# Half of the attention weights turned by VectorE and two DMAs instead of TensorE, in a 16-head attention stage

## The chip, the core and the metric

The kernel runs on one core of one Trainium2 chip. The time is device microseconds (us) of that core, for one whole execution of the program. Three timed runs of the kernel before took 1644.7 to 1644.83 us, median 1644.71. The profile shows a separate execution of the same program with a span of 1645.5 us.

## What is computed

The reference is a two-layer block over 512 positions of width 1024, followed by a second block, all in fp32. The change lies in the attention of the first layer, which in the reference is, cut to what matters:

```python
mod_x = silu_c @ mod_w[i] + mod_b[i]                 # 6144 values, used as shifts, scales and gates
q = (rmsnorm(h @ w_dq, g_q) @ w_uq)                  # 16 heads of 64 + 32 (the 32 are rotated)
k = concat([ckv @ w_uk, k_pe]); v = ckv @ w_uv       # 768 keys: 256 of the context, 512 of x
s = einsum('bqhd,bkhd->bhqk', q, k) * scale          # 512 queries x 768 keys, for each head
p = softmax(s, axis=-1)
o = einsum('bhqk,bkhd->bqhd', p, v)                  # 64 columns for each head
x = x + g1 * (o @ w_o)
```

The rest of the reference (two feed-forward blocks, a long convolution, a state-space branch and a pooling branch) is computed by parts of the program that the change does not touch.

## The kernel before

Each engine runs a list of instructions written out by hand; engines wait for each other through counted semaphores (`S["name"]`), and each list is executed in its order. A matrix product in fp32 precision is three products of rounded parts (`mm3`, lines 2442 to 2446): high by high, high by low, low by high.

The attention stage handles one head after another; with `head(h)` TensorE finishes head h and computes the scores of head h+1. For TensorE (lines 2836 to 2867) it is: transposes of the weights of head h; four score tiles of head h+1, each of 128 queries by 768 keys, with pieces of projections and more transposes between them; in even heads the key projection of the next pair; then `value(h)`, the product of the turned weights with V. A score tile takes two of the four PSUM banks 0 to 3, so tile qt+2 waits until the exponential of tile qt has read its banks (`sexp`, line 2772).

For each score tile VectorE takes the row maximum (`maximum`, line 3568), ScalarE the exponential with its row sum (`exponential`, line 3085), and VectorE the reciprocal of the sum (`inverse_sum`, line 3575), before it goes to the next maximum. The weights are multiplied by the reciprocal by GpSimd for tiles 0 to 2 (line 2374) and by ScalarE for tile 3 (line 3114). They stand with queries on the partitions (`PR`, two buffers, for even and odd heads); the product with V needs keys on the partitions, so TensorE turns 24 blocks of 128x128 for each head into PSUM (`turn_blocks`, line 2780), and ScalarE copies them to `PT` (`turn_copy`, line 3094). At the end of a head VectorE writes the low part of the head's output (`out_lo`, line 3581), which needs `value(h)` and ScalarE's high part.

VectorE has two more jobs there. It computes rows of the modulation, each a product of a 128x1024 piece of `mod_w` with the vector c and a sum (`mod_rows`, line 3519). Rows 0 to 27 are computed in heads 0 to 13, two in each; SyncE loads each piece (512 KB) into one of two buffers MR0 and MR1 once the row two before it is done (`mod_load`, line 2194). And between heads 14 and 15 it computes angles for the state-space branch (`prepare_angles`, line 3672). After the heads comes the output projection "wo", in eight tiles: `linear("wo", j)` waits until the residual of tile j-2 is added by VectorE (line 2457).

All DMAs of this stage are issued by SyncE, in the order of its list (lines 2244 to 2264). Which head is which matters: heads with h mod 4 equal to 1 carry the projection of the rotated part and heads with h mod 4 of 2 or 3 that of query pairs; heads 4, 8 and 12 have one such product only.

## Time and profile before

| | |
|---|---|
| median of 3 timed runs | 1644.71 us (1644.7 to 1644.83) |
| span of the profiled execution | 1645.5 us |
| TensorE busy | 1633.9 us, 99% |
| VectorE busy | 1043.6 us, 63% |
| ScalarE busy | 571.0 us, 35% |
| GpSimd busy | 1026.5 us, 62% |
| mean granted TensorE clock | 0.997 |
| DMA, mean over the span | 134 GB/s |

The profiled execution's own time is its span, 0.8 us above the median of the timed runs. The stage of the heads goes from 112.9 us, where head 0 begins, to 316.8 us, where the last product with V ends. Shares over the whole span say little of it: whether an engine is waited for there has to be read from that stretch. An idle time in square brackets stands before an instruction, with the engine and line that ended it.

### The profile page before, as it was taken

What the parts mean: (1) busy time and instruction counts of PE and PEld (TensorE: products, weight loads), DVE (VectorE), ACT (ScalarE), POOL (GpSimd) and SP (SyncE); (2) the same over time, 40 slices, a digit from 0 to 9 for tenths busy, and PEclk for the clock granted to TensorE, in tenths of its full rate; (3) what the DMA queues carried; (4) which work ended last, traced back from release to release, by engine and by line L of the source; (5) the groups of instructions that cost most, each with busy time, mean ns of one, the idle gap of its engine ahead of it and who ended that gap; (6) DMA issues with size and microseconds to landing.
All of it is one profiled execution on the core that took longest, in us unless ns stands there. A gap on an engine that the chain in (4) does not pass through costs nothing.

```text
span 1645.5 us, 24018 instructions
## 1 busy us (share of the span) xinstructions
PE 1633.9 (99%) x8950; PEld 1364.2 (83%) x8950; DVE 1043.6 (63%) x1537; ACT 571.0 (35%) x1017; POOL 1026.5 (62%) x656
## 2 busy tenths in 40 slices
PE   9999999999999999999999999999999999999998
PEld 7887778798888888889887798888888898888887
DVE  3567777677877865635487566655558359746173
ACT  3467777633233232203344243222222121123111
POOL 3455766656666766575579456666676645567663
PEclk9999999999999999999999999999999999999999
DMA  9234335232269863435322233344434253223332
GB/s 371 87 90 129 111 106 165 79 93 96 89 211 320 298 225 103 141 137 172 120 90 65 77 99 102 125 156 140 153 106 143 97 214 120 65 84 103 91 101 90
DMA packets 59095, 220.61 MB, mean 134 GB/s; under 512 B 6849, under 2 KB 9153, under 8 KB 55682
## 3 DMA queue, kind: packets, MB, share of 16 engines
q1 hardware_dynamic: 53826, 204.96, 38.2%
q10 hardware_dynamic: 5184, 14.49, 2.3%
q8 instruction: 57, 0.93, 0.2%
q14 instruction: 28, 0.23, 0.0%
HBM read 201.07 MB, written 14.16 MB: 131 GB/s over the span
## 4 chain that ended last, share of the span: by engine, by line
PE 95%; DVE 4%; ACT 0%; issue 0%; DMA 0%; DVEq 0%; SPq 0%; ACTq 0%
PE PS L2444 28%; PE PS L2446 28%; PE PS L2445 28%; PE PS L2821 3%; PE PS L2783 2%; PE PS L1012 1%; PE PS L2430 1%; PE PS L1785 1%; PE PS L2595 1%; DVE SC L3572 0%; DVE WA L1990 0%; PE PS L1791 0%; DVE MR L3522 0%; PE PS L2720 0%; PE PS L2721 0%
## 5 line engine op out<-in xcount | busy, mean ns | idle before, releaser
L2354 POOL TENSOR_TENSOR WL<-RAW,WH 128x1024 fp32r<-128x1024 f32 (+3 forms) x211 | 542.8, 2572 | 17.6
L2444 PE MATMUL PS<-HH,WH 128*128 128x512 f32 (+1 forms) x1340 | 507.5, 379 | 0.0
L2446 PE MATMUL PS<-HH,WL 128*128 128x512 f32 (+1 forms) x1340 | 502.9, 375 | 0.0
L2445 PE MATMUL PS<-HL,WH 128*128 128x512 f32 (+1 forms) x1340 | 502.9, 375 | 0.0
L2351 POOL TENSOR_SCALAR WH<-RAW 128x1024 fp32r<-128x1024 f32 (+3 forms) x211 | 239.4, 1134 | 287.8 <-PE PS L2446 276.5
L2444 PEld LDWEIGHTS PS<-HH,WH 128*128 128x128 f32 x1340 | 252.2, 188 | 50.7 <-issue 6.2
L2446 PEld LDWEIGHTS PS<-HH,WL 128*128 128x128 f32 x1340 | 252.2, 188 | 45.9
L2445 PEld LDWEIGHTS PS<-HL,WH 128*128 128x128 f32 x1340 | 252.3, 188 | 43.9
L2379 POOL TENSOR_SCALAR PR<-PR,SC 128x768 f32<-128x768 f32 x47 | 107.3, 2292 | 66.7 <-DVE SC L3579 66.3
L2444 PE MATMUL PS<-HIDH,WH 128*128 128x512 f32 (+1 forms) x396 | 145.3, 367 | 0.0
L2445 PE MATMUL PS<-HIDL,WH 128*128 128x512 f32 (+1 forms) x396 | 144.8, 366 | 0.0
L2446 PE MATMUL PS<-HIDH,WL 128*128 128x512 f32 (+1 forms) x396 | 144.7, 366 | 0.0
L2350 POOL TENSOR_TENSOR SC<-ONES 1x1 f32<-1x1 f32 x100 | 24.9, 249 | 180.1 <-PE PS L2446 177.7
L3278 ACT ACTIVATE ZG<-PS,PAR 128x512 f32<-128x512 f32 x44 | 34.3, 779 | 166.3 <-PE PS L2446 166.3
L2444 PEld LDWEIGHTS PS<-HIDH,WH 128*128 128x128 f32 x396 | 74.6, 188 | 12.6 <-issue 0.5
L2446 PEld LDWEIGHTS PS<-HIDH,WL 128*128 128x128 f32 x396 | 74.7, 189 | 12.1
L2445 PEld LDWEIGHTS PS<-HIDL,WH 128*128 128x128 f32 x396 | 74.7, 189 | 12.1
L3792 DVE SCALAR_TENSOR_TENSOR ZG<-PS,PAR,ZG 128x511 f32<-128x511 f32 x44 | 33.0, 750 | 72.2 <-ACT ZG L3278 71.9
L3572 DVE TENSOR_REDUCE SC<-PS 128x1 f32<-128x768 f32 x64 | 61.1, 955 | 23.1 <-PE PS L2446 22.5
L3681 DVE SCALAR_TENSOR_TENSOR X<-PS,MOD,X 128x512 f32<-128x512 f32 x26 | 19.5, 749 | 87.6 <-PE PS L2446 87.6
L3091 ACT ACTIVATE PR<-PS,SC 128x768 f32<-128x768 f32 x64 | 57.8, 903 | 44.3 <-DVE SC L3572 44.1
L3530 DVE CUSTOM_DVE_ANT_0 MRF<-MRF,PS 128x1024 f32<-128x1024 f32 x52 | 62.5, 1211 | 2.9 <-DMA MRF<-in_modw 2.7
(532 smaller groups left out, 2894.6 us busy)
## 6 DMA issues: line engine op xcount, KB each, us to landing
RAW<-in_wup SPq DMA_DIRECT2D x88, 512.0 KB, 3.6
MRF<-in_modw SPq DMA_DIRECT2D x52, 512.0 KB, 4.8
RAW<-in_wdn SPq DMA_DIRECT2D x32, 704.0 KB, 4.1
MR<-in_modw SPq DMA_DIRECT2D x28, 512.0 KB, 3.6
RAW<-in_whin SPq DMA_DIRECT2D x24, 512.0 KB, 3.5
MK<-in_modk SPq DMA_DIRECT2D x8, 1024.0 KB, 10.9
RAW<-in_wo SPq DMA_DIRECT2D x8, 512.0 KB, 4.2
hy_hs<-HST ACTq DMA_DIRECT2D x4, 1024.0 KB, 4.0
```

The lines of the kernel that those rows point to most:

```text
L2351: pool.tensor_scalar(WH[s][:, 0:n], raw[:, 0:n], 1.0, 0.0, ALU.mult, ALU.add).then_inc(tile_hi, 1)
L2354: pool.tensor_tensor(WL[s][:, 0:n], raw[:, 0:n], WH[s][:, 0:n].bitcast(F32), ALU.subtract).then_inc(tile_split, 1)
L2379: pool.tensor_scalar(PR[h % 2][:, qt, :], PR[h % 2][:, qt, :], RSUM[:, c:c + 1], None, ALU.mult).then_inc(S["pnorm"], 1)
L2444: pe.matmul(out, wh, xh, start=first, stop=False)
L2445: pe.matmul(out, wh, xl, start=False, stop=False)
L2446: return pe.matmul(out, wl, xh, start=False, stop=last)
L2821: m = pe.matmul(PS[VH * half:VH * half + VH, out_bank(h), 0:256], V[:, kt, v], PT[:, kt, tok(half)], start=kt == 0, stop=kt == 5)
L3091: act.activation(PR[h % 2][:, qt, :], wide(2 * (qt % 2), LK), ACT.Exp, bias=NMX[:, c:c + 1], scale=1.0, accum_out=SUMS[:, c:c + 1]).then_i ...
L3278: act.activation(buf[:, :], bank(first_bank(2 * o + half)), ACT.Identity, scale=par_at("fcw", i + (l * 3 * NUP + NUP + KF * half + o)), bi ...
L3530: dve.tensor_tensor_reduce(MRF[b][:, :], MRF[b][:, :], wide(6, D), 1.0, 0.0, ALU.mult, ALU.add, MOD[:, 16 + r:17 + r]).then_inc(S["mod_use ...
L3572: dve.tensor_reduce(NMX[:, c:c + 1], wide(2 * (qt % 2), LK), AX.X, ALU.max, negate=True).then_inc(S["smax"], 1)
L3792: link(dve.scalar_tensor_tensor(buf[:, 1:L], bank(bk)[:, 0:L - 1], w0, buf[:, 1:L], ALU.mult, ALU.add))
```

## The change

Of each head, query tiles 0 and 1 are no longer turned by TensorE (`BLOCKED = 2`). The exponential of these tiles writes its keys in another order: column c*192 + t*32 + j holds key 128t + 4j + c. VectorE then transposes the 32x32 blocks of each 128x768 tile in place (`block_turn`). SyncE writes both tiles to a buffer in HBM (`blocks_out`, 384 KB each), waits until both have landed and until the product with V of the head before is done, and reads them back with one DMA that puts 1024 pieces of 768 bytes on 128 partitions (`blocks_in`, 768 KB in all). The product with V reads these from `PB` and the turned tiles 2 and 3 from `PT`. TensorE turns 12 blocks for each head instead of 24, in three groups of four (`turn(h, 0)` and `turn(h, 1)` at the start, `turn(h, 2)` after the second score tile), and these wait for all of tiles 2 and 3, while before the first six waited for tile 2 only. ScalarE copies three times for each head instead of six.

The modulation rows are spread anew: rows 0 to 4 before head 0, rows 5 and 6 in head 0, two in each odd head up to 13, three in head 14 and four in head 15; none in even heads from 2 to 12. `prepare_angles` stands behind head 15. X is loaded again in two halves, at heads 14 and 15. Some semaphores are merged, with no change in what is waited for.

```diff
+BLOCKED = 2
+PRE_ROWS = 5
-        PT = r.put("PT", [P, 6, L])
+        PB = r.put("PB", [P, BLOCKED, 4, 6, 32])
+        PT = r.put("PT", [P, 6, P * (4 - BLOCKED)])
...
+            def blocks_out(h, qt):
+                sp.wait_ge(S["turned"], BLOCKED * h + qt + 1)
+                sp.dma_start(d_blocks[h % 2, qt, :, :], PR[h % 2][:, qt, :]).then_inc(S["blocks_out"], 16)
+            def blocks_in(h):
+                sp.wait_ge(S["pv"], h + 1)
+                sp.wait_ge(S["blocks_out"], 16 * BLOCKED * (h + 1))
+                sp.dma_start(PB[:, :, :, :, :].rearrange("p i m t j -> p (i m) (t j)"),
+                             d_blocks[h % 2].rearrange("i (m k) (c x) -> (k c) (i m) x", m=4, c=4)
+                             ).then_inc(S["blocks_in"], 16)
...
+            for r in range(4):
+                mod_load(16 + r)
+                if r == 1:
+                    head_weights(2)
+            for h in range(16):
...
+                if h % 2 and h < 15:
+                    mod_load(16 + PRE_ROWS + 1 + h)
+                    mod_load(16 + PRE_ROWS + 2 + h)
...
+                elif h == 14:
+                    sp.wait_ge(S["rope"], 512)
+                    x_again(0)
+                    mod_load(16 + EARLY - 7)
+                elif h == 15:
+                    mod_load(16 + EARLY - 5)
+                    mod_load(16 + EARLY - 4)
+                for qt in range(BLOCKED):
+                    blocks_out(h, qt)
+                if h > 13:
+                    mod_load(16 + EARLY + 3 * h - 48)
+                blocks_in(h)
+                if h == 0:
+                    for r in range(4, PRE_ROWS + 2):
+                        mod_load(16 + r)
+            x_again(1)
+            mod_load(16 + EARLY - 2)
+            mod_load(16 + EARLY - 1)
...
+            def turn(h, n):
+                if n == 0:
+                    pe.wait_ge(S["pnorm"], 3 * h + 2)
+                    if h == 0:
+                        pe.wait_ge(S["kready"], key_hi_at(0) + 2)
+                    else:
+                        pe.wait_ge(S["pt"], 4 * h + 1)
+                if n == 2:
+                    pe.wait_ge(S["pt"], 4 * h + 2)
+                for kt in (2 * n, 2 * n + 1):
+                    for qt in range(BLOCKED, 4):
+                        q = (kt % 2) * 256 + (qt - BLOCKED) * P
+                        m = pe.transpose(PS[:, 6 + n % 2, q:q + P], PR[h % 2][:, qt, kt * P:(kt + 1) * P], IDENT[:, :])
+                m.then_inc(S["s_tr"], 1)
...
+                pe.wait_ge(S["blocks_in"], 16 * (h + 1))
                 for kt in range(6):
-                    pe.wait_ge(S["pt"], 7 * h + kt + 2)
-                    for half in range(2):
-                        m = pe.matmul(PS[VH * half:VH * half + VH, out_bank(h), 0:256], V[:, kt, v],
-                                      PT[:, kt, tok(half)], start=kt == 0, stop=kt == 5)
+                    pe.wait_ge(S["pt"], 4 * h + kt // 2 + 2)
+                    pe.matmul(PS[0:VH, out_bank(h), 0:256].rearrange("p (i m j) -> p i m j", i=2, m=4), V[:, kt, v],
+                              PB[:, :, :, kt, :], start=kt == 0, stop=kt == 5)
+                    m = pe.matmul(PS[VH:2 * VH, out_bank(h), 0:256], V[:, kt, v], PT[:, kt, :], start=kt == 0, stop=kt == 5)
...
+                if qt < BLOCKED:
+                    out, src = out.rearrange("p (c t j) -> p c t j", c=4, t=6), src.rearrange("p (t j c) -> p c t j", t=6, c=4)
...
+            def block_turn(h, qt, i=0, per=0):
+                dve.wait_ge(S["pnorm"], i * (3 * per) + (3 * h + qt if h else qt + 1))
+                dve.transpose(PR[h % 2][:, qt, :], PR[h % 2][:, qt, :]).then_inc(S["turned"], 1)
...
                 if h < 15:
                     inverse_sum(h + 1, 3, i, per)
+                    block_turn(h + 1, 0, i, per)
...
                 if h % 2:
                     row(1)
+                if h in (14, 15):
+                    row(2)
+                if h == 15:
+                    row(3)
+                if h < 15:
+                    block_turn(h + 1, 1, i, per)
                 out_lo(h, i, per)
```

Two places show how the lists move: the start of head 0 on two engines, and the end of the heads on VectorE.

SyncE's list where the first modulation rows are loaded, before. MR is the buffer of a modulation row, RAW that of a weight tile.

```order
L2170 ISA [waits tile_split]
L2170 DMA RAW_53<-in_wheven 128x1280
L2196 ISA
L2197 ISA [waits s_mod_used]
L2197 DMA MR_93<-in_modw 128x1024
L2196 REGISTER_ALU
L2197 ISA [waits s_mod_used]
L2197 DMA MR_94<-in_modw 128x1024
```

The same place in the changed kernel. PR are the weights, PB their turned blocks.

```order
L2214 DMA MR_94<-in_modw 128x1024 [waits s_mod_used]
L2214 DMA MR_95<-in_modw 128x1024 [waits s_mod_used]
L2174 DMA RAW_53<-in_wheven 128x1280 [waits tile_split]
L2214 DMA MR_94<-in_modw 128x1024 [waits s_mod_used]
L2214 DMA MR_95<-in_modw 128x1024 [waits s_mod_used]
L2201 DMA pr_blocks<-PR_72 128x768 [waits s_turned] x2
L2207 DMA PB<-pr_blocks 128x8x192 [waits s_blocks_out,s_pv]
L2214 DMA MR_94<-in_modw 128x1024 [waits s_mod_used]
```

Four rows are loaded first, and the load of row 4, the last line, now stands behind the DMA that reads the blocks of head 0 back.

VectorE's list from the last reciprocal of head 0's scores, before. TENSOR_REDUCE is a maximum, here the first of head 1's scores; ISA with MR is a modulation row.

```order
L3579 RECIPROCAL SC<-SC 128x1 [waits s_sexp] x2
L3572 TENSOR_REDUCE SC<-PS 128x1 [waits s_s_ready]
L3522 ISA MR_93,SC<-MR_93,CB 128x1024 [waits s_mod_in0]
L3522 ISA SC 128x1
L3579 RECIPROCAL SC<-SC 128x1 [waits s_sexp]
```

The same place in the changed kernel.

```order
L3610 RECIPROCAL SC<-SC 128x1 [waits s_sexp]
L3625 STREAM_TRANSPOSE PR_72<-PR_72 128x768 [waits s_pnorm] x2
L3553 ISA MR_94,MOD<-MR_94,CB 128x1024 [waits s_mod_in0]
L3553 ISA MOD 128x1
L3553 ISA MR_95,MOD<-MR_95,CB 128x1024 [waits s_mod_in1]
L3553 ISA MOD 128x1
L3553 ISA MR_94,MOD<-MR_94,CB 128x1024 [waits s_mod_in0]
L3553 ISA MOD 128x1
L3603 TENSOR_REDUCE SC<-PS 128x1 [waits s_s_ready]
```

Two transposes and the modulation rows 2, 3 and 4 now stand ahead of the first maximum of head 1's scores.

VectorE's list from the last reciprocals of head 15's scores, before. HL is the low part of a head's output, S are the angles; the lines between the first and the last of the angles are left out here.

```order
L3579 RECIPROCAL SC<-SC 128x1 [waits s_sexp] x2
L3587 TENSOR_TENSOR HL<-PS,HH 64x256 [waits s_ohi] x2
L1398 TENSOR_SCALAR S_139<-PAR 128x16
...
L1507 TENSOR_SCALAR S_139<-S_139 128x16 [waits s_dchain]
L3587 TENSOR_TENSOR HL<-PS,HH 64x256 [waits s_ohi,s_s5d]
L3587 TENSOR_TENSOR HL<-PS,HH 64x256 [waits s_ohi]
```

The same place in the changed kernel; of the four modulation rows of head 15 the first is shown.

```order
L3610 RECIPROCAL SC<-SC 128x1 [waits s_sexp] x2
L3625 STREAM_TRANSPOSE PR_73<-PR_73 128x768 [waits s_pnorm]
L3553 ISA MR_95,MOD<-MR_95,CB 128x1024 [waits s_mod_in1]
L3553 ISA MOD 128x1
L3625 STREAM_TRANSPOSE PR_73<-PR_73 128x768 [waits s_pnorm]
L3618 TENSOR_TENSOR HL<-PS,HH 64x256 [waits s_ohi] x2
L3553 ISA MR_94,MOD<-MR_94,CB 128x1024 [waits s_mod_in0]
...
L3618 TENSOR_TENSOR HL<-PS,HH 64x256 [waits s_ohi] x2
L1402 TENSOR_SCALAR S_140<-PAR 128x16 [waits s_mod_used]
```

The low part of head 15's output stood behind the angles and now stands ahead of them, behind four modulation rows; two transposes with a modulation row between them have come in behind the reciprocals.

## Rows read from the trace of the kernel before

**Rows 1.** The page, chain that ended last, shares of the span.
```profile
PE 95%; DVE 4%; ACT 0%; issue 0%; DMA 0%; DVEq 0%; SPq 0%; ACTq 0%
```

**Rows 2.** Chain of waits, 200 to 235 us: start, length, engine, what.
```profile
208.23 1.02 PE PS L2783 x8
...
213.19 0.44 PE PS L2783 x4
```

**Rows 3.** Timeline of VectorE, head 7: start, length, engine, line, what, idle before.
```profile
210.35 0.96 DVE L3572 TENSOR_REDUCE SC<-PS 128x1 f32<-128x768 f32 x1 [0.58 <-PE PS L2446]
...
216.75 0.16 DVE L3579 RECIPROCAL SC<-SC 128x1 f32<-128x1 f32 x1 [1.06 <-ACT PR L3091]
216.89 0.96 DVE L3572 TENSOR_REDUCE SC<-PS 128x1 f32<-128x768 f32 x1
...
218.99 1.20 DVE L3522 CUSTOM_DVE_ANT_0 MR<-MR,CB 128x1024 f32<-128x1024 f32 x1
...
220.73 0.88 DVE L3587 TENSOR_TENSOR HL<-PS,HH 64x256 f32 x2 [0.53 <-ACT HH L3111]
222.16 0.96 DVE L3572 TENSOR_REDUCE SC<-PS 128x1 f32<-128x768 f32 x1 [0.56 <-PE PS L2446]
```

**Rows 4.** Timeline of VectorE, the first maximum in heads 1, 2, 5, 13, 14.
```profile
130.84 0.96 DVE L3572 TENSOR_REDUCE SC<-PS 128x1 f32<-128x768 f32 x1
...
142.16 0.88 DVE L3587 TENSOR_TENSOR HL<-PS,HH 64x256 f32 x2 [1.42 <-ACT HH L3111]
143.22 0.96 DVE L3572 TENSOR_REDUCE SC<-PS 128x1 f32<-128x768 f32 x1 [0.18 <-PE PS L2446]
...
182.99 0.96 DVE L3572 TENSOR_REDUCE SC<-PS 128x1 f32<-128x768 f32 x1 [0.56 <-PE PS L2446]
...
287.56 0.96 DVE L3572 TENSOR_REDUCE SC<-PS 128x1 f32<-128x768 f32 x1 [0.57 <-PE PS L2446]
...
300.05 0.96 DVE L3572 TENSOR_REDUCE SC<-PS 128x1 f32<-128x768 f32 x1 [0.80 <-PE PS L2446]
```

**Rows 5.** DMA issues of the page: KB each, median us from issue to landing.
```profile
RAW<-in_wdn SPq DMA_DIRECT2D x32, 704.0 KB, 4.1
MR<-in_modw SPq DMA_DIRECT2D x28, 512.0 KB, 3.6
...
hy_hs<-HST ACTq DMA_DIRECT2D x4, 1024.0 KB, 4.0
```

**Rows 6.** DMA issues by the DMA view, same columns.
```profile
X<-in_x SPq DMA_DIRECT2D x2, 1024.0 KB, 6.2
...
s_cs<-COW ACTq DMA_DIRECT2D x4, 256.0 KB, 2.1
```

**Rows 7.** Timeline of VectorE, start of head 0.
```profile
109.19 0.16 DVE L3579 RECIPROCAL SC<-SC 128x1 f32<-128x1 f32 x1 [1.87 <-ACT PR L3091]
115.04 0.96 DVE L3572 TENSOR_REDUCE SC<-PS 128x1 f32<-128x768 f32 x1 [5.69 <-PE PS L2446]
115.92 2.63 DVE L3522 CUSTOM_DVE_ANT_0 MR<-MR,CB 128x1024 f32<-128x1024 f32 x1
```

**Rows 8.** Timeline of TensorE, the last product with V and the fourth "wo" tile.
```profile
314.02 2.81 PE L2821 MATMUL PS<-PT,V 128*64 128x256 f32 x24
...
327.11 0.39 PE L2444 MATMUL PS<-HH,WH 128*128 128x512 f32 x1
```

**Rows 9.** Timeline of VectorE, end of the heads and "wo".
```profile
310.27 0.16 DVE L1398 TENSOR_SCALAR S<-PAR 128x16 f32<-128x16 f32 x1
...
318.11 0.88 DVE L3587 TENSOR_TENSOR HL<-PS,HH 64x256 fp32r<-64x256 f32 x2
...
320.60 0.75 DVE L3681 SCALAR_TENSOR_TENSOR X<-PS,MOD,X 128x512 f32<-128x512 f32 x1 [0.98 <-PE PS L2446]
321.87 0.75 DVE L3681 SCALAR_TENSOR_TENSOR X<-PS,MOD,X 128x512 f32<-128x512 f32 x1 [0.52 <-PE PS L2446]
...
330.39 0.74 DVE L3681 SCALAR_TENSOR_TENSOR X<-PS,MOD,X 128x512 f32<-128x512 f32 x1
```

More of the change, by code:

```diff
@@ L3123, in head @@
                 turn_copy(h, 0, i, per)
+                if h % 4 == 0 and per:
+                    mod_store(i)
                 for kt in range(1, 6):
[L3125 removed]
+                    if kt == 1 or kt == 3:
+                        turn_copy(h, (kt + 1) // 2, i, per)
                     if kt == 1 and h % 4 == 3 and h < 12:
@@ L3145, in head @@
                     query_hi(3)
-                if h % 2 and h < 14:
-                    mod_store(2 * h - 2, 4, i, 2 * per)
             rope_hi(0)
```

175 lines of the change are left out of this document (83 added, 92 removed).

## Prediction, written before the changed kernel ran

> **What bounds the kernel now.** I read the page first. The chain that ended last is TensorE for 95% of the span [rows 1], so a change pays if it takes work off TensorE and no other engine takes its place. Then the chain of waits in the stretch of the heads, for the price of what goes: a group of four transposes holds the chain 0.44 us, the first eight of a head 1.02 us [rows 2]. Then VectorE's timeline of one head, since the share of 63% over the span says nothing of the heads. In head 7 it is in a chain with ScalarE: maximum, exponential (it waits 1.06 us for it), reciprocal, next maximum [rows 3]. From the first maximum to the fourth go 210.35 to 216.89, so 6.54 us for three tiles, 2.18 each. TensorE's own pace there is a score tile, a projection piece and a group of transposes, and it is the same: the maximum at 222.16 waited 0.56 us for TensorE, but the middle ones come with no wait for it [rows 3]. So in the heads the two bounds lie on one another. That decides: taking 0.44 us off TensorE for a tile doesn't shorten a tile, because the chain of VectorE and ScalarE keeps its 2.14 us (0.96 maximum, 1.06 wait, 0.16 reciprocal, less the overlap).
>
> **What the change takes away.** Three groups of four transposes in each of 16 heads: 16 x 3 x 0.44 = 21.1 us of TensorE. It is worth that only where TensorE is waited for. ScalarE's three copies for each head lie beside the exponentials and are worth nothing by themselves.
>
> **The new VectorE work.** Two transposes of 128x768 for each head, which the trace does not show. The nearest row is the maximum over 128x768, 0.96 us, with 0.88 to the next instruction's start [rows 3 and 7]; I take 0.88. From below, the 128x1024 modulation row takes 1.20 [rows 3], so 0.9 for 768, and if the transpose ran at twice that speed 0.45; from above, the same row took 2.63 once, beside GpSimd's work [rows 7], so 2.0. The Trainium skill ("Vector Engine (DVE) Microarchitecture Reference", section 3.8) has the 32x32 transpose at one element per cycle and lane, an estimate of 0.80 us for 768 at 0.96 GHz; by it the sum would be some 2 us smaller, and no run here shows it yet.
>
> **Heads 1 to 12.** The transposes stand behind the last reciprocal, and behind them the low part of the output and then the first maximum of the next head. Nothing hides them but VectorE's idle time there. In head 7 that is 0.53 + 0.56 = 1.09 us [rows 3]; the work is 1.76, and the three tiles go 0.1 faster: +0.6 us. The same for heads 3 and 11. In head 1 the idle time is 1.42 + 0.18 = 1.60 [rows 4], so +0.1; the same for 5 and 9. Even heads lose both modulation rows (2.4 us) and gain 1.76 us. About half of what goes lay in the waits for the exponential, so -0.35 each. Four heads together: 0.6 + 0.1 - 0.7 = 0, against 182.99 - 130.84 = 52.15 us before [rows 4]. Three such rounds: 0. The 21 us of TensorE become idle time in front of VectorE.
>
> **The round trip.** 384 KB out: between 2.1 us for 256 KB and 4.0 for 1024 KB [rows 5 and 6], so 2.4. 768 KB in: 512 KB take 3.6 and 704 KB 4.1 [rows 5], so 4.3 by that slope; I take 4.6 because its 1024 pieces are short. 1024 KB took 6.2 beside other transfers [rows 6]; pieces of 768 bytes are not in the trace, and I put the ends at 4.1 and 9. With 0.2 us for the two issues the round trip is 7.2 us. The second tile is turned some 0.9 us before the next head's first maximum (the low part lies between), so the product with V can start 6.3 us after that maximum, ends 2.8 later (9.1) [rows 8], and the next first maximum comes 2.1 us behind the head's first transposes (210.35 - 208.23) [rows 2 and 3]: 11.2, against 12.4 in which VectorE goes round. The cover is 1.2 us; a longer round trip is paid in every odd head and most even ones.
>
> The Trainium skill ("DMA: Bandwidth & Descriptors", the fixed cost of a DMA) puts 2.0 us on each transfer before its bytes; by it the trip is 2.9 + 3.8 = 6.7 us, an estimate that keeps the cover, and the sum the same. The skill ("VectorE: DVE Perf Modes", rules for kernel authors) sends a full 128x128 transpose to TensorE where PSUM will do, which speaks against the change but has no price here.
>
> **The start of head 0.** This is the first loss. VectorE is free at 109.35 [rows 7]. Two transposes to 111.1, the DMA out lands at 113.6, the DMA in is issued, and only behind it the load of modulation row 4. That load waits for 768 + 512 KB: by the slope above 3.6 + 768 x 0.0026 = 5.6 us, so 119.5. Row 4 takes 1.2, and the first maximum of head 1 stands behind it: 120.8 in place of 115.04 [rows 7]. TensorE has two score tiles of room in PSUM and then stops. Price +5.8 us. If the load shares the engines evenly it lands 1.5 us sooner: 4 to 6.5.
>
> **Head 13.** From its first maximum to that of head 14 go 300.05 - 287.56 = 12.49 us [rows 4]. In these heads the maxima stand ahead of the reciprocals, so VectorE is not tied to 2.14 us a tile, and TensorE's saving shows. VectorE then sets 11.8 (its last reciprocal at 7.9, then 0.88 + 1.2 + 0.88 + 0.9): -0.7 us.
>
> **Heads 14 and 15.** Head 15 has no scores behind its transposes, so little lies between the products of heads 14 and 15, and the round trip is bare. From head 14's first maximum: last reciprocal 8.64 in head 7 [rows 3], less one group of 0.44, 8.2; transpose, modulation row, transpose 3.0: 11.2; round trip 7.2: 18.4, and the product starts there. Before it started at 314.02 - 300.05 = 13.97 [rows 4 and 8]. Price +4.5 us.
>
> **The output projection.** Modulation rows 26 and 27 are loaded behind the DMA in of head 15 and 1 MB of X, so at some 22.2 and 23.5 us on the same count; with their two sums the low part of head 15's output ends at 25.6, 4.4 us behind the product's end (21.2). Then come the angles, 318.11 - 310.27 = 7.84 us [rows 9], which stood before it. The bias and columns 0.6, two residuals 1.5: the second residual ends 4.4 + 7.8 + 0.6 + 1.5 = 14.3 us behind the product. Tile 3 of "wo" waits for it; before it started 327.11 - 316.83 = 10.3 behind [rows 8]. Tile 4 waits for the third residual, 8.5 us later (331.13 - 322.62) [rows 9], at 22.8. Before it came a tile behind tile 3, at 10.3 + 5.5 = 15.8. Price +7.0 us; between 4.0 (tile 3 alone) and 8.4 (no slack behind).
>
> **The sum.** 5.8 + 0 - 0.7 + 4.5 + 7.0 = 16.6 us on the profiled span of 1645.5: 1662.1. The timed median lies 0.8 under the span: 1661.
>
> **Rivals.**
> 1. The round trip is longer. For it: its pieces are short and the read goes behind two writes and beside 512 KB loads. At 10.2 us instead of 7.2, 1.8 us are uncovered; in 12 heads 1.8 x 12 = 22, and 3 more at head 15: 1661 + 25 = 1686. With transposes at 2.0 us instead of 0.88 the loss is 2 x 1.1 x 13 = 29: 1690. Against both: the nearest rows. Chance 0.19.
> 2. The ends cost what I say, but VectorE is not the bound inside the heads, because TensorE's earlier scores let it catch up (a transpose at 0.45 would do this): 13 heads gain up to 1.3 us, 17 in all: 1661 - 17 = 1644, no change. Against it: the strict order of reciprocal and next maximum. Chance 0.05 for within 0.2%.
> 3. Faster: the same gain, and the load of row 4 and the angles find cover too: 1645 - 21 + 4.5 = 1628. For it: 21 us of TensorE do go, and PE is 95% of the chain. Against it: rows 7 and 9. Chance 0.09.
> 4. The forecast, 1648 to 1676: 0.67.
>
> A change under 0.2% (3.3 us) can't be told from none here. So faster 0.09, same 0.05, slower 0.86. The range reaches from 1648, half of the gain in the heads, to 1686, the long round trip.
>
> **What would show it.** In the profile after: a first maximum of head 1 at about 120.8; rounds of four heads of about 52 us, with TensorE idle in front of scores, released by the exponentials, and VectorE without idle time at a head's end; transposes of about 0.96 us; DMAs of 2.4 and 4.6 us; TensorE idle some 6 us before the last product with V, released by the DMA; tile 3 of "wo" waiting for a residual. I am wrong if rounds of four heads take under 49 us, or if the product with V waits for the DMA in every head.

## The result and the profile after

The changed kernel takes 1675.21 us (median of 4, 1674.92 to 1675.67), the kernel before it 1644.77 (4 runs beside it, 1644.7 to 1644.91). The ratio is 1.0183, with a 95% interval of 1.0168 to 1.0197: 30.4 us slower. The prediction was 1661, in a range of 1648 to 1686. The direction and the places were right; the size was short by 14 us.

The span of the profiled execution grew from 1645.5 to 1673.9 us, by 28.4. The other 2.4 of the stretches below are in the profile of before: there TensorE's granted clock is 0.78 and 0.53 in the two stretches of 5 us from 10 to 20 us, and 1.00 in both after the change. So head 0's last reciprocal stands at 109.19 before [rows 7] and at 106.68 after. In the other profiled executions of the kernels of this study it stands between 106.5, where that clock is 1.00 in both stretches, and 110.7, where it is 0.65 and 0.50. To keep that out, I compare stretches and not times from the span's start:

| stretch | before | after | loss | forecast |
|---|---|---|---|---|
| S: last reciprocal of head 0's scores to the first maximum of head 1's | 5.85 | 13.75 | 7.9 | 5.8 |
| H: first maximum in head 1 to that in head 13 | 156.72 | 162.22 | 5.5 | 0 |
| first maximum in head 13 to that in head 14 | 12.49 | 12.07 | -0.4 | -0.7 |
| V: first maximum in head 14 to head 15's product with V | 13.97 | 19.15 | 5.2 | 4.5 |
| W: from there to the third product of wo's last part (the first 128x256 residual) | 32.48 | 45.72 | 13.2 | 7.0 |

The first maximum in head 0 to that in head 1 takes 15.80 before and 15.19 after, -0.6. Sum: 7.9 - 0.6 + 5.5 - 0.4 + 5.2 + 13.2 = 30.8. After the last of these stretches nothing is lost.

The chain that ended last, on the page of the changed kernel; before it was TensorE for 95% [rows 1].

```profile
PE 86%; DVE 7%; DMA 4%; issue 2%; ACT 1%; DVEq 0%; SPq 0%; ACTq 0%
```

And its DMA issues, to be read beside [rows 5]: the blocks out and in, and the modulation rows, which took 3.6 us before and share the engines with the blocks now.

```profile
MR<-in_modw SPq DMA_DIRECT2D x28, 512.0 KB, 6.2
pr_blocks<-PR SPq DMA_DIRECT2D x32, 384.0 KB, 2.6
PB<-pr_blocks SPq DMA_DIRECT2D x16, 768.0 KB, 4.8
```

**The start.** VectorE's timeline of the changed kernel at head 0, the counterpart of [rows 7]:

```profile
106.76 1.82 DVE L3625 STREAM_TRANSPOSE PR<-PR 128x768 f32<-128x768 f32 x2
108.50 1.18 DVE L3553 CUSTOM_DVE_ANT_0 MR<-MR,CB 128x1024 f32<-128x1024 f32 x1
...
111.06 1.93 DVE L3553 CUSTOM_DVE_ANT_0 MR<-MR,CB 128x1024 f32<-128x1024 f32 x1 [1.37 <-DMA MR<-in_modw]
...
119.28 1.23 DVE L3553 CUSTOM_DVE_ANT_0 MR<-MR,CB 128x1024 f32<-128x1024 f32 x1 [6.28 <-DMA MR<-in_modw]
...
120.43 0.95 DVE L3603 TENSOR_REDUCE SC<-PS 128x1 f32<-128x768 f32 x1
```

Two transposes take 1.82 us together. Row 4, at 119.28, waited 6.28 us for its load, and the first maximum of head 1 comes right behind it. SyncE's timeline has the reason; the load of row 4 is the first of the three in the last line:

```profile
107.74 1.18 SPq L2201 DMA_DIRECT2D pr_blocks<-PR  x2
113.40 0.38 SPq L2207 DMA_DIRECT2D PB<-pr_blocks  x1
113.83 7.04 SPq L2214 DMA_DIRECT2D MR<-in_modw  x3
```

**The heads.** In 11 of the first 14 heads the product with V waits for nothing. In three it waits for the blocks, and these are the heads with h mod 4 = 3 (TensorE's timeline, heads 3, 7 and 11):

```profile
169.93 0.40 PE L2848 MATMUL PS<-PB,V 128*64 128x256 f32 x1 [0.76 <-DMA PB<-pr_blocks]
...
225.70 0.66 PE L2848 MATMUL PS<-PB,V 128*64 128x256 f32 x1 [3.39 <-DMA PB<-pr_blocks]
...
278.96 0.40 PE L2848 MATMUL PS<-PB,V 128*64 128x256 f32 x1 [1.14 <-DMA PB<-pr_blocks]
```

What TensorE waited for in the stretch H says who bounds it. The columns are: who waited for whom, us in total, times, longest. Before the change it is one line, so TensorE itself was the bound there:

```profile
PE PS L2444 <- ACT PR L3091: 0.5, 3, 0.2
```

After it, five lines add up to 18.3 us; the first two are the blocks and the exponential that frees the banks of a score tile:

```profile
PE PS L2848 <- DMA PB<-pr_blocks: 5.3, 3, 3.4
PE PS L2482 <- ACT PR L3120: 4.8, 5, 1.0
```

The chain of waits through head 7 has the whole round trip on the path (start, length, what):

```profile
214.26 0.97 DVE PR L3625
215.25 4.37 DMA pr_blocks<-PR
219.68 5.77 DMA PB<-pr_blocks
```

That is 10.1 us where the forecast had 7.2. In an undisturbed head the two take 2.3 and 4.7 to 4.8. Ahead of this one lie 2.2 MB of loads, issued from 203.88 on, and behind the read four DMAs of rotated queries were issued at once; no run takes these away one by one.

**The end.** The chain of waits of the changed kernel from 321 us on:

```profile
326.89 8.47 DMA MR<-in_modw
...
337.10 0.43 DVE HL L3618
...
338.01 2.23 DVE S L1404
340.27 0.98 DVE S L1406
...
341.49 2.27 DVE S L1407
...
344.00 1.07 DVE S L1409
...
345.30 2.25 DVE S L1414
...
351.13 1.42 DVE X L3743 x2
```

Modulation row 27 needs the buffer of row 25, its load takes 8.47 us beside X and the blocks, and the low part of head 15's output stands behind it. Then come the angles (S), 12.94 us for what took 7.84 before [rows 9], and only then the first residual. TensorE waits twice:

```profile
337.58 0.62 PE L2482 MATMUL PS<-HH,WH 128*128 128x512 f32 x1 [2.77 <-DVE HL L3618]
...
352.59 0.80 PE L2482 MATMUL PS<-HH,WH 128*128 128x512 f32 x1 [5.63 <-DVE X L3743]
```

Three single instructions of the angles take 2.2 us where their likes take 0.17 to 0.2, and two take 1.0 us. GpSimd's timeline in the same stretch shows what they stand beside: subtractions (low parts of weight tiles) and rounding steps of 1.04 us (high parts). The first of the three ends at 340.24 and the subtraction beside it at 340.20, the second (341.49) at 343.76 and its subtraction at 343.72.

```profile
337.82 2.38 POOL L2392 TENSOR_TENSOR WL_third<-RAW,WH_third 128x1024 fp32r<-128x1024 f32 x1
340.18 1.04 POOL L2389 TENSOR_SCALAR WH<-RAW 128x1024 fp32r<-128x1024 f32 x1
341.31 2.41 POOL L2392 TENSOR_TENSOR WL<-RAW,WH 128x1024 fp32r<-128x1024 f32 x1
```

Before the change the angles met less of this. One instruction of 0.17 us took 0.95 beside a rounding step of 1.05 us, and two that take 0.38 together took 2.43 beside a subtraction that starts at 313.99 (VectorE's timeline of before):

```profile
312.98 0.95 DVE L1412 TENSOR_SCALAR S<-S 128x16 int32<-128x16 f32 x1
313.97 2.43 DVE L1392 TENSOR_TENSOR S<-S 128x16 f32<-128x16 f32 x2
```

### The profile page after: what moved, and what is told of

Same layout as the page of the kernel before. It is cut to its first block, busy times and chain, and to the rows that moved or that the text cites. A ratio compares the mean times of both kernels' runs of the same rounds, so it can differ in the third digit from the quotient of the medians.

```text
span 1673.9 us, 23555 instructions
## 1 busy us (share of the span) xinstructions
PE 1622.2 (97%) x8758; PEld 1349.1 (81%) x8758; DVE 1070.2 (64%) x1569; ACT 547.4 (33%) x965; POOL 1026.1 (61%) x657
## 4 chain that ended last, share of the span: by engine, by line
PE 86%; DVE 7%; DMA 4%; issue 2%; ACT 1%; DVEq 0%; SPq 0%; ACTq 0%
PE PS L2482 26%; PE PS L2484 26%; PE PS L2483 26%; DMA MR<-in_modw 1%; PE PS L2848 1%; DVE SC L3603 1%; DMA PB<-pr_blocks 1%; DMA pr_blocks<-PR 1%; PE PS L1016 1%; DVE PR L3625 1%; PE PS L1789 1%; DVE MR L3553 1%; PE PS L2468 0%; DVE WA L1994 0%; DVE HL L3618 0%
## 5 line engine op out<-in xcount | busy, mean ns | idle before, releaser
L2392 POOL TENSOR_TENSOR WL<-RAW,WH 128x1024 fp32r<-128x1024 f32 (+3 forms) x211 | 549.3, 2603 | 17.6
L2389 POOL TENSOR_SCALAR WH<-RAW 128x1024 fp32r<-128x1024 f32 (+3 forms) x211 | 234.4, 1111 | 287.4 <-PE PS L2484 273.3
```

The costliest lines, as they stand in the source:

```text
L2389: pool.tensor_scalar(WH[s][:, 0:n], raw[:, 0:n], 1.0, 0.0, ALU.mult, ALU.add).then_inc(tile_hi, 1)
L2392: pool.tensor_tensor(WL[s][:, 0:n], raw[:, 0:n], WH[s][:, 0:n].bitcast(F32), ALU.subtract).then_inc(tile_split, 1)
```

## The experiments

Twelve kernels ran. The times of one kernel scatter more here than before the change: TensorE's mean granted clock lies between 0.988 and 0.994 in nearly all timed runs of these kernels, 0.996 to 0.999 in those of before, and the last kernel shows a run at 0.998 beside four at 0.993 and 0.994. Each ratio is against runs of the kernel before that were made beside it; their medians are 1644.77 to 1646.65 us. All twelve kernels, like the changed one, are slower than it, by intervals that lie clear of 1. Between themselves a difference of a few microseconds can be the clock's, so the verdicts rest on the stretches of the table above, in the profiled executions:

| kernel | median us, ratio to before (95%) | S | H | V | W |
|---|---|---|---|---|---|
| before | 1644.77 | 5.85 | 156.72 | 13.97 | 32.48 |
| after | 1675.21, 1.0183 (1.0168 to 1.0197) | 13.75 | 162.22 | 19.15 | 45.72 |
| row4_early | 1672.41, 1.0172 (1.0152 to 1.0193) | 10.12 | 159.45 | 18.86 | 44.80 |
| early_read | 1669.87, 1.0148 (1.0131 to 1.0165) | 12.19 | 157.58 | 16.61 | 47.54 |
| max_first | 1670.03, 1.015 (1.0131 to 1.0169) | 13.39 | 157.03 | 18.71 | 45.68 |
| rows_back | 1663.07, 1.0102 (1.0085 to 1.0119) | 5.86 | 167.47 | 17.04 | 33.95 |
| no_turns | 1663.9, 1.0111 (1.0094 to 1.0128) | 14.79 | 151.04 | 18.99 | 44.45 |
| no_turns_early_read | 1663.2, 1.0111 (1.0091 to 1.013) | 11.35 | 151.52 | 15.13 | 48.23 |
| rows_before_x | 1672.75, 1.0166 (1.0149 to 1.0183) | 13.59 | 159.45 | 19.09 | 42.83 |
| last_head_tensore | 1671.18, 1.015 (1.0133 to 1.0167) | 13.44 | 161.46 | 14.25 | 44.94 |
| angles_alone | 1671.06, 1.0144 (1.0129 to 1.016) | 13.54 | 161.68 | 18.87 | 40.30 |
| no_turns_max_first | 1663.69, 1.0106 (1.0091 to 1.0122) | 14.57 | 150.39 | 19.46 | 44.28 |
| combined | 1665.48, 1.0112 (1.0098 to 1.0126) | 9.32 | 166.96 | 21.66 | 32.51 |
| combined_2 | 1662.32, 1.0097 (1.008 to 1.0114) | 4.96 | 166.39 | 14.61 | 32.86 |

Each stretch is from one profiled execution. S, V and W repeat within 1.1 us in kernels whose edit doesn't touch them. H scatters more: in the four kernels that leave that part as it is (row4_early, rows_before_x, last_head_tensore, angles_alone) it is 159.45, 159.45, 161.46 and 161.68, against 162.22 in the changed kernel. Part of it is one DMA: the wait in head 7 is 3.39 us in the changed kernel and 1.16 to 2.06 in those four. I compare with 159.45, the lowest; a difference of H under 3 us shows little by itself.

**row4_early**

```diff
+                if h == 0:
+                    mod_load(16 + 4)
                 blocks_in(h)
```

> The changed kernel with one DMA moved: the load of modulation row 4 is issued ahead of the DMA that reads the blocks of head 0 back, no longer behind it. My theory: row 4's wait (6.28 us idle on VectorE before 119.28) is the whole of the first loss, so the first maximum of head 1 comes at 115.4 to 116 in place of 120.43, TensorE's wait of 7.09 us goes with it, and the time falls by 5 us, to about 1670. Rival: the product with V of head 0 and its blocks would hold TensorE at that place anyway; then less than 2 us come back.

S fell by 3.6 us, not 5. The load of row 4 did come 5 us earlier, and VectorE waited 1.32 us for it instead of 6.28. But now rows 3 and 4 took 2.17 and 2.54 us instead of 1.2 (its timeline):

```profile
111.81 2.17 DVE L3555 CUSTOM_DVE_ANT_0 MR<-MR,CB 128x1024 f32<-128x1024 f32 x1 [1.13 <-DMA MR<-in_modw]
...
115.32 2.54 DVE L3555 CUSTOM_DVE_ANT_0 MR<-MR,CB 128x1024 f32<-128x1024 f32 x1 [1.32 <-DMA MR<-in_modw]
```

GpSimd's subtraction of a 128x1280 weight tile ran from 113.00 to 116.78; row 4 ended 1.1 us behind its end, about its own length.

**early_read**

```diff
                 sp.wait_ge(S["pv"], h + 1)
-                sp.wait_ge(S["blocks_out"], 16 * BLOCKED * (h + 1))
...
+                blocks_in(h)
                 for qt in range(BLOCKED):
                     blocks_out(h, qt)
...
-                blocks_in(h)
```

(The read takes its bytes from a weight tensor. TensorE's first transposes of a head wait, in this kernel alone, for the DMAs out of the head before.)

> The round trip is taken out of the path: the 768 KB read into PB takes its bytes from a weight tensor in HBM (same 1024 pieces of 768 bytes), is issued ahead of the two DMAs out and doesn't wait for them; the product with V of tiles 0 and 1 is therefore computed from other numbers. All bytes are still moved and all transposes are done. My theory: the product with V waited for the DMA 0.76 us in head 3, 3.39 in head 7, 1.14 in head 11 and 2.1 in head 14, and row 4's load no longer stands behind the read: 5 us at the start and 5.3 in the heads come back, little at the end (there the modulation rows 26 and 27 end later than the product); 1675 - 12 = 1663. Rival A: the trip binds in every head; then 15 to 20 us more come back, 1645. Rival B: the trip binds nowhere and only the start comes back: 1670.

All waits of the product with V in heads 3, 7 and 11 are gone. H fell 4.6 us against the changed kernel, but only 1.9 against row4_early, where these waits come to 3.2 us. So the trip costs the heads 2 to 5 us. Rival A fell. The median fell by 5.3 us where 12 were expected, since the start did not come back: the read was issued 0.4 us behind row 3's load and ahead of row 4's, these loads took 5.9 and 8.0 us, and row 3 itself took 3.79 us beside GpSimd's subtraction.

**max_first**

```diff
-                    inverse_sum(h + 1, 0, i, per)
                     maximum(h + 1, 1, i, per)
+                    inverse_sum(h + 1, 0, i, per)
```

(and the same for tiles 1 and 2.)

> The changed kernel with another order on VectorE in heads 0 to 12: each maximum stands ahead of the reciprocal of the tile before it, as it does in heads 13 and 14. My theory (VectorE and ScalarE in a chain of 2.12 us a tile hold TensorE in the heads): the wait of 1.06 us for each exponential is used for the next maximum, TensorE's saving of 1.3 us a head shows, and the time falls by about 10 us to 1665, less than 16 because the round trip then becomes late in most heads. Rival: the round trip already sets the length of the heads; then the time stays within 2 us of 1675 and the wait moves to the product with V in every head. A third: the weights are scaled later by GpSimd, and the time gets longer.

H fell 2.4 us against row4_early, no more than H scatters, and 5.2 against the changed kernel; 10 were expected. The strict order of reciprocal and maximum is at most a part of the bound. The third possibility shows too: before the first transposes of a head TensorE now waits for GpSimd's scaling, 3.3 us in five heads.

**rows_back**

```diff
-PRE_ROWS = 5
+PRE_ROWS = 0
...
-                        r = PRE_ROWS + 2 + h - 1 + k
...
+                    r = 2 * h + k
...
             head(14)
-            head(15)
             dve.wait_ge(S["mod_used"], 16 + EARLY)
             prepare_angles()
+            head(15)
```

(`r` is the row that head h computes; SyncE's loads move with the rows.)

> The changed kernel with the modulation rows as before the change: rows 2h and 2h+1 in head h for heads 0 to 13, none ahead of head 0, none in heads 14 and 15, and the angles between heads 14 and 15. Blocks are turned by VectorE and DMA as in the changed kernel. My theory: start and end lose their price (5.4 us at head 0; behind the last product with V 13.2 us, from rows 26 and 27 whose loads are late, and from the angles), and the 12 rows that come back into the even heads stand in the waits for exponentials and cost 0.2 us each: 1675 - 18 + 2.5 = 1659. Rival: in the even heads VectorE has no room and each row costs its 1.2 us: 12 x 1.2 = 14 more, 1671.

The median of 1663.07 lies between the theory's 1659 and the rival's 1671. S is as before to 0.01 us, and W lost 11.8 of its 13.2. So all of the loss at the start, and nearly all behind the last product with V, is due to the new spread of the modulation rows and not to the turning. The angles took 4.96 us here, from 322.69 to 327.65, while GpSimd was idle. But H is 8.0 us above row4_early's and 5.3 above the changed kernel's: the 12 rows cost 0.4 to 0.7 us each, two to three times my figure. It is also 10.7 us above the kernel before, which has the same rows in the same heads, so the turning by itself costs the heads that much; its new spread of the rows hid half of it.

**no_turns**

```diff
-                sp.wait_ge(S["turned"], BLOCKED * h + qt + 1)
+                sp.wait_ge(S["pnorm"], 3 * h + qt if h else qt + 1)
...
-                dve.transpose(PR[h % 2][:, qt, :], PR[h % 2][:, qt, :]).then_inc(S["turned"], 1)
```

> The changed kernel without VectorE's 32 transposes: the DMAs out wait for the scaled weights themselves. The product with V of tiles 0 and 1 is computed from weights whose 32x32 blocks are not turned; everything else, the round trip too, is as in the changed kernel. Theory A (VectorE's transposes stand in the strict piece at a head's end, behind the last exponential and ahead of the next head's first maximum, and give back what TensorE saves): the heads fall by what TensorE has to spare, about 5 us in four heads, so rounds of 48 instead of 53, and 1.8 us more at the start and at the end: 1675 - 15 - 3 = 1657. Theory B (the round trip and the waits for exponentials hold the heads, the transposes are hidden): 3 us or less in all, 1672.

H fell to 151.04: 8.4 us less than in row4_early, 0.7 for each head, and now 5.7 below the kernel before. Theory A holds in kind, and in size for about half: the median fell by 11.3 us, where it said 18 and theory B at most 3. But 15.8 us of TensorE's work (12 x 3 x 0.44) are gone from these 12 heads, and TensorE's waits in the stretch H say where the other 10 stay:

```profile
PE PS L2831 <- ACT PR L3148: 6.0, 6, 1.4
PE PS L2482 <- ACT PR L3120: 3.0, 3, 1.0
PE PS L2482 <- DVE HL L3618: 1.0, 3, 0.3
```

The first line is 6.0 us before the first transposes of a head, which wait for tile 3 to be scaled (before, the first six waited for tile 2 only, and TensorE did not wait there at all); the second is 3.0 for the exponential that frees the banks of a score tile, the third 1.0 for the low part of an output. The same view of row4_early, with the transposes:

```profile
PE PS L2484 <- ACT PR L3122: 5.4, 6, 1.0
PE PS L2484 <- DVE HL L3620: 3.3, 6, 0.8
PE PS L2850 <- DMA PB<-pr_blocks: 3.2, 3, 1.4
PE PS L2484 <- issue: 2.7, 3, 1.6
PE PS L2833 <- ACT PR L3150: 2.3, 5, 0.9
```

Sums: 151.0 - 10.0 = 141.0, and 159.45 - 16.9 = 142.5. What is left is TensorE's work, and it is nearly what the saving promised: 156.72 - 15.8 = 140.9. How much of the 6.0 us is due to the added wait for tile 3 no run shows. In this trace GpSimd had scaled tile 2 between 0.7 and 0.8 us before ScalarE had scaled tile 3, so an estimate from these rows is that some 4 us would go if the first transposes waited for tile 2 alone; the rest is TensorE coming earlier, with less work behind it.

**no_turns_early_read**

> Both costs taken away: no transposes on VectorE, and the read into PB ahead of the DMAs out and from a weight tensor, so that no product with V waits for it. The product of tiles 0 and 1 is computed from other numbers. What is left of the change is TensorE's saving, the copies that ScalarE no longer makes, and the new spread of the modulation rows. Theory A: as without transposes, and 5 us more from the waits of the product with V and 1 to 2 at the start, 1651. If the heads do not fall below 50 us for four even here, it is neither of the two costs but the row of score, maximum, exponential and reciprocal that holds them, 1668.

(The edits of no_turns and early_read together.) H is 151.52, no less than in no_turns, where no product with V waited for the blocks in any of these heads. So without transposes the round trip costs the heads nothing: it is late only because the transposes stand ahead of it. The expected 5 us from these waits did not come; the median of 1663.2 is the one of no_turns (1663.9), and the theory of 1651 fell. H is 50.5 us for four heads, not below the 50 that the expectation asked for, and TensorE's waits are those of no_turns again: 6.0 us at the heads' starts, 3.1 and 1.0.

**rows_before_x**

```diff
-            x_again(1)
             mod_load(16 + EARLY - 2)
             mod_load(16 + EARLY - 1)
+            x_again(1)
```

> The changed kernel with one order changed on SyncE behind head 15: the loads of modulation rows 26 and 27 are issued ahead of the second half of X (1 MB), not behind it. My theory: row 27's load took 8.5 us there beside X and the blocks and holds the low part of head 15's output (337.5, 5.6 us behind the end of the product with V); it comes 4 us earlier, and with it the angles and the first residual: 1675 - 4 = 1671. Rival: the loads stay slow because the read of the blocks is still under way; less than 1.5 us.

W fell by 2.9 us of the 4 that were said, and the median by 2.5. Row 27's load took 4.46 us instead of 8.47.

**last_head_tensore**

```diff
-                turn(h, 0)
-                turn(h, 1)
+                if h < 15:
+                    turn(h, 0)
+                    turn(h, 1)
+                else:
+                    turn_last(0)      # tiles 0 and 1 by TensorE too
+                    turn_last(1)
```

> Head 15 alone is turned by TensorE (24 blocks, six copies by ScalarE), with no transposes on VectorE and no DMAs for it; heads 0 to 14 as in the changed kernel. My theory: the last product with V starts 14 us behind head 14's first maximum as before the change (19.15 in the changed kernel), 5 us earlier, but the low part of the output still waits for rows 26 and 27, whose loads get only 2 to 3 us earlier since 1.5 MB of traffic goes: 1675 - 2.5 = 1672.5. Rival: the product sets the end; then the whole 5 us come back, 1670.

V is 14.25 us, as before the change, and W did not grow: V and W together fell by 5.7 us. The median fell by 4.0 us, between the theory's 2.5 and the rival's 5; the stretches speak for the rival: the 1.5 MB that aren't moved let the rows' loads come about as much earlier as the product. Row 27 landed 5.7 us behind the product's start, 6.3 in the changed kernel.

**angles_alone**

```diff
-                pool.tensor_tensor(WL[s][:, 0:n], raw[:, 0:n], WH[s][:, 0:n].bitcast(F32), ALU.subtract)
+                pool.tensor_scalar(WL[s][:, 0:n], raw[:, 0:n], 1.0 / 4096, 0.0, ALU.mult, ALU.add)
```

> The changed kernel with another instruction on GpSimd for the low parts of the weight tiles 2 to 7 of wo: one with a single input (the raw weights times a constant) in place of the subtraction of two tensors. The low parts are therefore other numbers. My theory: the angles took 12.94 us in the changed kernel, 7.84 before and 4.96 where GpSimd was idle, because single instructions of VectorE with SBUF operands alone stand still for as long as a subtraction on GpSimd runs (they end at its end, three times, 2.2 us each). Then the angles take 5 us here, the first residual comes 8 us earlier, the third residual and the tiles of wo 6 to 8: 1675 - 7 = 1668. Rival: GpSimd stops VectorE with any instruction on SBUF; then the angles keep about 12 us and the time stays.

The result lies between the two. The angles took 8.8 us (338.55 to 347.32) and W fell by 5.4. Instructions of the angles still stopped, but for no longer than GpSimd's shorter instruction, 1.06 us. VectorE's timeline and then GpSimd's:

```profile
339.01 0.90 DVE L1404 TENSOR_SCALAR S<-S 128x16 f32<-128x16 f32 x1
339.95 1.12 DVE L1406 SCALAR_TENSOR_TENSOR S<-S 128x16 f32<-128x16 f32 x2
```

```profile
338.82 1.06 POOL L2393 TENSOR_SCALAR WL_third<-RAW 128x1024 fp32r<-128x1024 f32 x1
339.96 1.08 POOL L2389 TENSOR_SCALAR WH<-RAW 128x1024 fp32r<-128x1024 f32 x1
```

So a GpSimd instruction with one input stops them too; how long it runs is the price. There are five such stops, of 0.7 to 0.8 us.

The Trainium skill ("SBUF — State Buffer", "Who interferes with whom") says that VectorE and GpSimd share one pair of ports, which one holds for a whole instruction while the other is fully blocked, and that a VectorE instruction with two inputs in SBUF needs it against any GpSimd instruction that reads SBUF. By that rule, the traces of the angles agree: 2.2 us beside a subtraction of 2.4, 0.9 to 1.0 beside an instruction of 1.06, no stop with GpSimd idle. The traces do not agree for GpSimd's scaling of the weights, which reads SBUF too: a modulation row took its usual 1.22 us within it (last section), and the measurement decides.

**no_turns_max_first**

> No transposes on VectorE (the product of tiles 0 and 1 is computed from weights whose blocks are not turned) and each maximum ahead of the reciprocal before it. It asks what refuses the rest of TensorE's saving: from the first maximum of head 2's scores to that of head 14's go 156.7 us before the change, 162.2 after it, 157.0 with the maximum first and 151.0 without transposes; TensorE's 12 x 1.32 = 15.8 us would give 141. My theory: the two add up, since without transposes the maximum still waits behind the reciprocal and its exponential, 2.12 us a tile: 151.0 - 5 = 146, in all 1664 - 5 = 1659. Rival: the round trip or the turning of tile 3 at a head's start takes over; then no more than 2 us, 1662.

(The edits of no_turns and max_first together.) The theory fell and the rival holds: H is 150.39, 0.65 less than in no_turns. TensorE's wait of 6.0 us at a head's start only changed its name, from ScalarE's scaling of tile 3 to GpSimd's of tile 2, whose reciprocal now comes later.

**combined**

> All that the runs point to, blocks still turned by VectorE in heads 0 to 14: head 15 turned by TensorE, each maximum ahead of the reciprocal before it, modulation rows 0 to 3 before head 0, two in head 0, six in each four heads of 1 to 12 (odd heads and those that are multiples of four), two each in heads 13 and 14, row 4 loaded ahead of the blocks of head 0, the angles between heads 14 and 15, and the DMAs of the rotated queries in heads 4, 8 and 12 issued behind the read of the blocks. From the runs so far: start 3.5 us, heads 2.7 + 2 less 3 for the rows, product of head 15 5, behind it 12: 1675 - 22 = 1653, between 1648 and 1657, so still slower than before the change (1645). Rival: the parts don't add, since the rows and the angles are on one engine; 1660.

The edits of last_head_tensore, max_first and row4_early, with a spread of the rows and an order on SyncE as the expectation says. S and W came back as hoped, H and V did not, and the median is 1665.48 where 1653 was expected and 1660 by the rival. TensorE's timeline, heads 4 and 14:

```profile
182.24 0.66 PE L2871 MATMUL PS<-PB,V 128*64 128x256 f32 x1 [4.18 <-DMA PB<-pr_blocks]
...
323.82 0.66 PE L2871 MATMUL PS<-PB,V 128*64 128x256 f32 x1 [6.71 <-issue]
```

The loads of rows stood in SyncE's list ahead of the blocks out, and one of them waits for a row that VectorE computes between the two transposes. A wait in that list holds everything behind it. The DMAs out of heads 4 and 14 then took 5.3 to 7.1 us beside these loads (and beside half of X in head 14), where they take 2.3 in a quiet head.

**combined_2**

```diff
-                turn(h, 0)
-                turn(h, 1)
                 for qt in range(4):
                     score(h + 1, qt)
+                    if qt == 0:
+                        turn(h, 0)
+                        turn(h, 1)
```

(Cut to the order on TensorE; the rows and SyncE's order as the expectation says.)

> The combined kernel mended where its trace showed new waits: the product with V waited 4.2, 2.3 and 2.2 us for the blocks in heads 4, 8 and 12 and 6.7 in head 14, because the loads of modulation rows and of X stood ahead of the DMAs out. Here those loads are issued behind the read of the blocks of the head before, modulation row 3 moves into head 0 (row 27 into head 14), and TensorE takes the first score tile of the next head ahead of the turning of the head's tiles 2 and 3, so that it has work while tile 3 is scaled (0.7 to 1.1 us idle in seven heads). My theory: 15 of the DMA waits' 18 us go, of which some 12 were on the path, and 2 to 4 us come from the score tile: 1665 - 15 = 1650, still not below the kernel before the change (1645). Rival: the round trip stays late in most heads, since each head is shorter; 1658 or more.

The waits for blocks fell to 0.2 and 0.9 us and V to 14.61, S to 4.96. H stayed at 166.39, 9.4 above max_first, with no DMA in it: VectorE is busy 132.2 us of it, 125.2 in max_first, which is six rows more, and TensorE waits up to 1.9 us for ScalarE's copies and 1.4 for the low keys. I did not separate the rows from the new order of the first score tile. The forecast of 1650 fell. The profiled execution took 1654.8 us at a mean clock of 0.998, the other four 1661.6 to 1664.2 at 0.993 or 0.994: its trace has no wait of TensorE above 2.7 us in the heads. The other four are 6.8 to 9.4 us longer; where the clock fell in them no trace shows. No version beat the kernel before.

## Why the prediction was right, and where its sizes were off

**What bounds the heads.** It was right that TensorE's saving of 21 us would not show. That two bounds lay on one another is half right: VectorE had little room, but TensorE, with 0.5 us of waits in H, was the one that bound. The reason given for the refusal, a chain of VectorE and ScalarE of 2.14 us a tile, is only a part. By the runs the 12 heads of H go: -15.8 for TensorE's work, +10.0 in waits that appear with no transposes at all, 6.0 of them for tile 3 at a head's start; +8.4 for the transposes and the trip that starts behind them (row4_early against no_turns; 1.9 of it the trip); +2.8 up to this one execution. Of these, 2.0 are the slow DMA of head 7, and the clock behind it accounts for the rest: six pairs of products went 0.43 us apart instead of 0.21, some 1.3. The change lists a condition behind the 6.0 us, "these wait for all of tiles 2 and 3", and my sum had no term for it; that it causes about 4 of them is an estimate. The forecast's zero for these heads came out of parts that were wrong, and that it missed by no more than 5.5 us is luck.

**The transposes.** One takes 0.96 us in the trace and 1.82 for two, so 0.91 with the next start, against a forecast of 0.88. The Trainium skill's rate ("Vector Engine (DVE) Microarchitecture Reference", section 3.8) gave an estimate of 0.80; the measurement decides. Forecast for heads 1 to 12: 0; measured 5.5 in the profile and 2.7 to 5 in the four kernels with the same heads. The step that failed is "the cover is 1.2 us": it took the trip as 7.2 us in all heads. It is 2.3 + 4.8 in a quiet head, where the product with V did not wait, and up to 4.4 + 5.8 in heads 3, 7 and 11, where loads of 2.2 MB and the DMAs of rotated queries run beside it. In the other nine heads of H no product waited. That is the first rival's mechanism in three heads of twelve.

**The start.** The place and the cause were as said. The first maximum of head 1 came at 120.43, forecast 120.8, but that agreement is luck: VectorE was free 2.5 us earlier than in the profile of before. The size is 7.9, not 5.8. The term that was mis-sized is the time from the second transpose to the landing of the blocks, 4.8 us instead of 2.5, beside 1.6 MB of loads. The load of row 4 itself took 5.4 us, forecast 5.6.

**Head 13.** The stretch changed by -0.4 us, forecast -0.7.

**Heads 14 and 15.** The loss was 5.2 us, forecast 4.5, by the steps that were given: second transpose done at 11.4 behind the first maximum, forecast 11.2; round trip 7.7, forecast 7.2; product at 19.15, forecast 18.4. last_head_tensore took the loss all away.

**The output projection.** This is the term that was most wrong, 13.2 us against 7.0. The order of events up to tile 3 of wo was right: low part behind rows 26 and 27, angles behind it, tile 3 behind a residual. Tile 3 started 23.5 us behind the start of the product with V (352.59 - 329.06), and 13.1 before the change: 10.4 later, where the forecast's own steps give 4.0. Two sizes make the 6.4. The low part ended 5.7 us behind the product's end instead of 4.4, since row 27's load took 8.5 us (rows_before_x: W 2.9 us shorter). And the angles were priced by their row of before, 7.84 us, as if that were their length. It was 4.96 of work and stops of 2.05 and 0.8 beside GpSimd; in their new place they meet three subtractions, 6.2 us of stops, and two rounding steps, 1.7. That is 12.94, 5.1 more. What the step needed was GpSimd's timeline beside VectorE's, at the old place and at the new one.

The last step failed: "Tile 4 waits for the third residual, 8.5 us later". The third residual ended 4.2 us behind the second (356.72 - 352.54), and tile 4 did not wait. The 8.5 us of before held 7.2 of further angle instructions that met GpSimd (322.54 to 329.76); in the changed kernel they took 2.9 with GpSimd idle. In the place of that wait stands the clock. Behind the wait of 5.63 us tile 3 ran at the lower of the two levels for 5.3 us, 13 products 0.43 us apart instead of 0.23, which is 2.8 us. So 10.4 + 2.8 = 13.2, and that a wait that never came was priced at 3.0, near the clock's 2.8, is luck. Over all of W TensorE was busy 4.8 us longer for the same work, at a mean clock of 0.89 instead of 1.00 (before, then after; columns as in the last section):

```profile
314.02:346.50 32.48, 32.48 (x168) 26.77 (x168) 27.98 (x66) 9.81 (x17) 18.90 (x11) 1.00 0.30 87
329.06:374.78 45.72, 37.32 (x167) 29.98 (x168) 34.96 (x85) 9.07 (x15) 19.97 (x12) 0.89 0.35 121
```

**The rivals.** The long round trip held in kind for three heads, 5.3 us of waits where it was priced at 22. The gain of the heads that would have left the time unchanged did not come: H grew. That the load of row 4 and the angles find cover, as the faster rival wanted, was excluded by S and W.

## What to carry to other kernels

A wait that a new dependency adds on an engine (here: all transposes of a head on the slowest of four tiles) is a term of its own, also where the engine gets less work; look for it at the place where the engine has nothing else. Work that is moved is priced at its new place: the length in the old row includes what it collided with there. And small jobs that fill a busy engine's gaps (the modulation rows) should not be moved for a gain elsewhere before both places are priced: undoing only their new spread took back 19.7 us at the two ends, and cost 5 to 8 in the heads.

## What the runs showed of the hardware

**VectorE beside GpSimd.** Instructions of VectorE on 128x16 elements in SBUF, 0.17 us alone, last until the end of a GpSimd subtraction or rounding step that is running: 2.2 us, three times, and 1.0 us, twice. A modulation row of 1.2 us took 2.54, 2.63 [rows 7] and 3.79 beside a subtraction, and 1.93 and 2.17 beside a rounding step of 1.26; each ended 1.1 us behind GpSimd's end. It goes the other way too: where GpSimd's subtraction of 128x1280 started during a row, it took 3.78 us (112.01 in the changed kernel) instead of 2.94 in the kernel before. Not stopped, in the changed kernel, were the transposes (0.97 us at 146.27, within a subtraction of 145.35 to 148.03), and modulation rows beside GpSimd's scaling of the weights (1.22 us at 125.66, within 122.71 to 129.28).

**The clock behind a wait.** Most of TensorE's longer waits cost more than themselves. Granted clock and busy times of the changed kernel behind its waits of 7.09, 3.39 and 3.29 us and then during and behind that of 5.63 us (stretch, its length, busy times of PE, PEld, DVE, ACT and POOL, clock, DMA share, GB/s):

```profile
122.00:124.00 2.00, 1.54 (x4) 1.25 (x5) 1.46 (x4) 0.92 (x3) 1.29 (x1) 0.50 0.92 337
...
225.70:228.00 2.30, 2.30 (x12) 1.50 (x14) 2.30 (x4) 0.56 (x1) 2.22 (x2) 0.50 0.75 232
...
329.00:332.00 3.00, 2.94 (x25) 2.16 (x26) 0.00 (x0) 0.10 (x1) 0.00 (x0) 1.00 0.99 404
...
346.96:352.59 5.63, 0.00 (x0) 0.00 (x0) 5.01 (x21) 0.62 (x2) 0.55 (x1) 0.90 0.31 95
352.60:355.00 2.40, 2.40 (x6) 1.92 (x7) 1.99 (x13) 2.35 (x5) 0.00 (x0) 0.50 0.00 0
```

At 0.50 the clock is at 1.2 GHz, and a 128x512 product takes 0.63 us instead of 0.39. In the changed kernel it was so behind waits of 2.09 (head 14), 2.77, 3.39, 5.63 and 7.09 us. It was not behind one of 3.29 us (head 15) or 1.14 (head 11), nor behind one of 2.63 in combined_2. So the length of the wait alone does not decide, and these runs do not show what else does.

**A DMA next to others.** The same 384 KB took 2.3 to 5.3 us and the same 768 KB 4.6 to 6.3, from issue to landing, by what was in flight.
